# A transformer layer with two kinds of attention: the seam between its expansion stage and its attention stage, rearranged

## The chip, the cores and the metric

The kernel runs on one core of a Trainium2 chip. The metric is the device time of one execution in microseconds (us); the kernel before has a median of 3106.4 us over three runs (3103.69 to 3112.34).

## What is computed

One layer of a diffusion transformer over 2048 latent tokens of width 1024, with 256 context tokens as a prefix. All matrices are float32; the kernel splits operands into a high and a low part (`_hi`, `_lo`) and multiplies them in several passes to keep precision.

```python
u = x * (1 + m1) + m0;  h = u @ w_in                      # modulate, project
mq = rms_norm(h[cq]) @ w_uq                               # MLA queries, 6 heads of 64 + 32 (rope)
kv = rms_norm(h[ckv]) @ w_ukv                             # MLA keys and values, 6 heads
gq, gk = rms_norm(h[gq]), rms_norm(h[gk])                 # GQA, 6 query heads, 2 key heads of 64
q_pe, k_pe, gq, gk = apply_rope(...)
mo = block_attention(mq, m_k, m_v, 6)                     # softmax(q k^T * scale) v, 2304 keys
go = block_attention(gq, g_k, g_v, 2)
co = cb * short_conv(cc * ch, w_conv)                     # depthwise, width 3
y  = concat([mo, go, co]) @ w_o
x  = layer_norm(ALPHA * x + m2 * y)
x  = layer_norm(ALPHA * x + m5 * (relu((x*(1+m4)+m3) @ w1)**2 @ w2))
```

## The kernel before

The program is a row of stages, each a block in which the five engines (PE, ACT, DVE, POOL, SP) run streams written out by hand and meet through semaphores; a block ends for all engines together. `stage_modulate` and `stage_project` come first and leave their results in DRAM. The change touches the next two.

**`stage_expand` (line 616)** computes the MLA queries, keys and values from the compressed rows. It loops over four blocks b of 512 tokens (`NQB`). In each, PE makes three query tiles into the PSUM tile `ring`, then two rope tiles into `rope_ps` (12 matmuls), then three key tiles into `ring`, then, for b below 3, six value tiles (`VG`) into the two banks of `v_ps`. ACT copies each tile out as its high part (`item`, line 696; `values`, 703), DVE subtracts for the low part (731). For the rope tiles DVE multiplies by cosine and sine (749 to 752), POOL adds and subtracts (721, 722), ACT makes `ro_hi` (714), POOL `ro_lo` (725). SP stores everything to DRAM: `store_set` for queries and keys (`qn`, `kn`, line 662), `qr` (679), `vm` (682). It also loads what is missing: compressed rows, tables, and at b = 2 the first GQA head (`load_heads`: `gq`, `gk_ll`, `gv`; lines 842 to 844). A copy into a buffer waits on ACT or POOL until the store that last used it has landed. At the end SP waits for the landing of all stores and of the head's loads (from line 684 on), and so the block ends after them.

Beside this, 40 maxima are taken: softmax of the first attention block needs row maxima of its scores beforehand, so PE multiplies 128 queries by up to 512 keys into a bank (785) and DVE reduces it (737). All of them use the one bank `mx_ps`, except the last ten, which follow everything else in the two `v_ps` banks (`PLACES`, `ALONE`, `last_maxima`). The first needs `gq_first`, loaded late in the stage before.

**`stage_attend` (line 891)** runs 24 blocks of 1024 queries: two GQA blocks and two MLA blocks for each of six heads. A block has 18 steps kt. In each, PE makes scores into one of two pairs of banks (`scores`, 1419), ACT takes the exponential into one of ten probability tiles `pf` (1256), POOL or DVE adds it to a running denominator (1211, 1297); after each six steps PE multiplies the six tiles by the values (1435). Between the score matmuls stand the maxima of the blocks to come (`pair`, 1373, read by DVE in 1275); block 0 carries 27 of them, and from the twentieth on they are on MLA data, for which PE waits on `in_mh`. The negative maximum enters the scores as one more row, laid by `lay_first_row` (1384) for block 0 and by `turn_row`, an ACT copy and small DMAs (`move_row`) for the others. In some blocks (0 among them) PE also multiplies a strip of `w_ada` (`modulations`, 850) after step 11.

SP issues in this order before its loop: the shared rope keys `rk_hh` (four issues) and `rk_lm` (two), `load_m(0)` (the 22 high loads, 14 low loads and values of MLA head 0), `load_part(0)`, `load_wa(0)` (2 MB), `load_part(1)` (convolution inputs). POOL first fills pads of `max_row[1]`, `rk_lm` and `mq` (1159), eight operations, and PE and the row moves wait for all of them (`padded`).

The SBUF of the expansion's own tiles is used again by tiles of attention, `pf` and `rk_lm` among them.

## Time and profile before

| | us |
|---|---|
| median of three runs | 3106.4 |
| the profiled execution | 3108.44 |
| its span (first to last record) | 3106.6 |
| PE busy in the span | 2943.1 (95%) |
| DVE busy | 2291.2 (74%) |
| ACT busy | 1320.4 (43%) |
| POOL busy | 1399.5 (45%) |
| expansion, first to last matmul | 423 to 510 |
| attention, first work | 526.1 |

Times in the rows further down are us from the start of the span. PE is busy nearly everywhere, so what matters are the few stretches where it is not, and its clock: PEclk is the granted TensorE clock as a share of 2.4 GHz, 0.50 being 1.2 GHz. The DMA share is the mean busy share of the 16 DMA engines and can read a little over 1. A line with an idle time in brackets names what ended that idle time.

### The profile page before, as it was taken

How to read it: one execution, taken by the hardware profiler on the slowest of the kernel's cores; microseconds unless marked ns; L12 is line 12 of the kernel's file. 1: busy time of each engine (PE TensorE's matmuls, PEld its weight loads, DVE VectorE, ACT ScalarE, POOL GpSimd, SP SyncE). 2: the span in 40 equal slices, each digit the busy share in tenths (PEclk: the TensorE clock that was granted, in tenths of full speed). 3: DMA queues.
4: the chain of work that ended last, by engine and by line, in shares of the span. 5: the costliest groups of instructions: out<-in, count | busy, mean ns of one | idle time of the engine just before them, and what ended most of it. 6: DMA issues, size and time to landing. Idle time of an engine off the chain costs nothing. (4 is left out here: it accounts for less than half of the span.)

```text
span 3106.6 us, 43125 instructions
## 1 busy us (share of the span) xinstructions
PE 2943.1 (95%) x15760; PEld 2210.2 (71%) x15760; DVE 2291.2 (74%) x3178; ACT 1320.4 (43%) x1891; POOL 1399.5 (45%) x837
## 2 busy tenths in 40 slices
PE   5999966999999999999999969999999999999997
PEld 3889854566656556565657858887788888887886
DVE  4445454778787878878776888776877768888878
ACT  3222323344444444444442445555555544433441
POOL 1233313577786968766661234333333134223420
PEclk7999987999999999999999989999999999999999
DMA  6132379335343243433026876446444488887873
GB/s 257 59 89 76 98 244 274 103 70 130 93 108 86 52 92 84 90 93 76 8 95 237 287 275 242 157 152 263 179 152 157 172 324 302 293 294 293 296 289 141
DMA packets 252012, 526.64 MB, mean 170 GB/s; under 512 B 35568, under 2 KB 110832, under 8 KB 240624
## 3 DMA queue, kind: packets, MB, share of 16 engines
q1 hardware_dynamic: 245296, 498.33, 49.7%
q10 hardware_dynamic: 6528, 25.82, 2.1%
q8 instruction: 115, 1.88, 0.2%
q14 instruction: 73, 0.60, 0.1%
HBM read 363.19 MB, written 160.76 MB: 169 GB/s over the span
## 5 line engine op out<-in xcount | busy, mean ns | idle before, releaser
L1275 DVE TENSOR_REDUCE h_mpart<-a_mx 128x1 f32<-128x512 f32 x920 | 537.8, 632 | 169.4 <-PE a_mx L1373 156.6
L1211 POOL TENSOR_TENSOR a_acc_p<-a_acc_p,a_pf 128x1024 f32<-128x1024 f32 x240 | 578.7, 2411 | 166.8 <-ACT a_pf L1256 139.6
L1256 ACT ACTIVATE a_pf<-o_y 128x1024 f32<-128x1024 f32 x432 | 442.0, 1026 | 398.1 <-PE o_y L1419 392.6
L2430 PE MATMUL f_bank<-slots,f_wx 128*128 128x512 f32 x2304 | 532.8, 391 | 14.7 <-DMA slots<-s_uc 9.2
L2438 PE MATMUL f_bank<-slots 128*128 128x512 f32 x2352 | 539.5, 391 | 3.6 <-DVE slots L2209 3.6
L2438 PEld LDWEIGHTS f_bank<-slots 128*128 128x128 f32 x2352 | 443.4, 189 | 96.5 <-DVE slots L2209 4.3
L2430 PEld LDWEIGHTS f_bank<-slots,f_wx 128*128 128x128 f32 x2304 | 434.8, 189 | 107.6 <-DMA slots<-s_uc 11.2
L2376 POOL TENSOR_TENSOR f_work<-raw_rows 128x512 f32<-128x512 f32 x160 | 220.9, 1382 | 379.5 <-DVE f_wx L2202 367.7
L2385 POOL TENSOR_TENSOR f_y<-f_y,raw_rows 128x1024 f32<-128x1024 f32 x72 | 195.3, 2713 | 343.5 <-DMA raw_rows<-in_w 343.5
L2223 DVE TENSOR_TENSOR f_work<-f_work,f_bank 128x512 f32<-128x512 f32 x256 | 174.4, 681 | 134.1 <-ACT f_work L2101 123.3
L553 PE MATMUL p_main<-win_hi,u_hi 128*128 128x512 f32 (+2 forms) x528 | 197.9, 375 | 15.1 <-PEq L75 14.4
L2209 DVE TENSOR_TENSOR slots<-f_y,slots 128x1024 fp32r<-128x1024 f32 x98 | 151.3, 1544 | 64.1 <-ACT slots L2085 63.1
L553 PE MATMUL p_main<-win_hi,u_lo 128*128 128x512 f32 (+2 forms) x528 | 196.3, 372 | 0.0
L553 PE MATMUL p_main<-win_lo,u_hi 128*128 128x512 f32 (+2 forms) x528 | 196.2, 372 | 0.0
L1435 PE MATMUL a_o<-a_pf,a_v 128*64 128x512 f32 x864 | 192.8, 595 | 0.0
L1435 PE MATMUL a_o<-a_pf,h_gv 128*64 128x512 f32 x864 | 192.8, 595 | 0.0
L2085 ACT ACTIVATE slots<-f_y 128x1024 fp32r<-128x1024 f32 x98 | 104.0, 1061 | 197.5 <-POOL f_y L2385 186.4
L883 PE MATMUL o_y<-slots,low 128*128 128x512 f32 x768 | 180.2, 394 | 3.4 <-PEq L893 3.4
L2207 DVE TENSOR_TENSOR slots<-raw_rows,slots 128x1024 fp32r<-128x1024 f32 x98 | 159.6, 1628 | 25.9 <-ACT slots L2077 25.4
L883 PEld LDWEIGHTS o_y<-slots,low 128*128 128x128 f32 x768 | 143.9, 189 | 34.8 <-issue 5.4
L1419 PE MATMUL o_y<-h_gq,h_gk_hh 64*128 64x512 f32 x864 | 165.5, 406 | 0.2
L2202 DVE TENSOR_TENSOR f_wx<-f_work,f_wx 128x512 fp32r<-128x512 f32 x160 | 162.5, 1017 | 0.6
(279 smaller groups left out, 5101.1 us busy)
## 6 DMA issues: line engine op xcount, KB each, us to landing
raw_rows<-s_hx SPq DMA_DIRECT2D x112, 512.0 KB, 4.0
f_y<-in_w SPq DMA_DIRECT2D x104, 512.0 KB, 5.3
raw_rows<-in_w SPq DMA_DIRECT2D x72, 512.0 KB, 5.8
raw_rows<-in_w SPq DMA_DIRECT2D x32, 1024.0 KB, 4.9
s_hx<-stream SPq DMA_DIRECT2D x128, 256.0 KB, 2.7
s_hx<-f_work SPq DMA_DIRECT2D x96, 256.0 KB, 2.0
raw_rows<-in_w_ada SPq DMA_DIRECT2D x8, 2048.0 KB, 8.4
low<-s_mix SPq DMA_DIRECT2D x32, 512.0 KB, 5.6
```

Of the source, the lines that this page charges most:

```text
L553: mm = nc.tensor.matmul(main[:, b, 0:cn], lhs[s][:, k], rhs[:, k, c0:c0 + cn], start=(k == 0 and rhs is w_hi and lhs is u_hi), stop=(k == ...
L883: mm = nc.tensor.matmul(y[:, half, :], x_[s % 2][:, k], w_[k][:, half * 512:(half + 1) * 512], start=(k == 0 and n == 0), stop=(k == KD - ...
L1211: nc.gpsimd.tensor_tensor(acc[:, :], left[:, :], pf[(b * KT + kt) % NPF][:, :], ALU.add).then_inc(added_p, 1)
L1256: nc.scalar.activation(pf[n % NPF][:, :], sc[n % 2][:, :], ACT.Exp, scale=SCALES[0 if is_mla(b) else 1]).then_inc(exped, 1)
L1275: nc.vector.reduce_max(mpart[b % 2][:, s + 4 * half, k:k + 1], bank(("pair", c), half)[:, 0:CHUNKS[k][1]], AX.X).then_inc(mx_read, 1)
L1419: mm = nc.tensor.matmul(sc[n % 2][:, half * QB:(half + 1) * QB], w, y[strip, :], start=(m == 0), stop=(m == len(ops) - 1))
L1435: mm = nc.tensor.matmul(o_ps[half * DH:(half + 1) * DH, :], v[0 if is_mla(b) else 1][:, kt], pf[n % NPF][:, half * QB:(half + 1) * QB], st ...
L2223: nc.vector.tensor_tensor(t, t, bank[:, (NP * n + pos) % 8, :], plus(sign)).then_inc(c_set, 1)
L2376: nc.gpsimd.tensor_tensor(out, w1_part(n, first), w1_part(n, second), plus(sign)).then_inc(sum_set, 1)
L2385: nc.gpsimd.tensor_tensor(y1[cc % YN], y1[cc % YN], y2[k % Y2N], plus(sign)).then_inc(y_sum, 1)
L2430: mm = nc.tensor.matmul(by_pair(bank[:, m % 8, :]), w[:, k], x[s][:, :, k * P:(k + 1) * P], start=(k == 0 and j == 0), stop=(k == 3 and j ...
L2438: mm = nc.tensor.matmul(bank[:, 4 * (pr % 2) + tt, :], x[s][:, f, tok], y[s][:, 2 + f, :], start=(start and j == 0), stop=(stop and j == 2))
```

## The change

It does the following, in the expansion:

- PE makes the rope tiles first in each block, DVE multiplies them first, ACT makes `ro_hi` before the key tiles, and SP stores `qr` between the query and the key tiles.
- The maxima turn over three banks (`mx_ps` and the two of `rope_ps`): the query half of a block stays on one, keys and values use all three. Six of the last ten move into the ring of block 3, four remain at the end.
- In block 3 SP issues the `qn` stores and stops. The stores of `qr` and `kn` of that block are issued by attention's SP (`last_expanded`). Nobody waits for landings at the end of the block.
- The values `gv` are no longer among the first head's loads.

And in attention:

- The store semaphores live on. ACT waits for `vm` stores before probability tile 2, for `qr` before tile 5, for the others before tile 8; the ten tiles are taken in another order. PE waits for `gv` before its first value product and for the head's loads after `lay_first_row`.
- SP's order is: `gv`, the four stores, `load_wa(0)`, `load_part(0)`, `load_part(1)`, a wait for the landing of all stores, `rk_hh`, the 22 high loads of MLA head 0; then, after the row move of block 1, `rk_lm` and the low loads with the values.
- POOL fills the `rk_lm` pads after its eighth addition of block 0; GQA blocks no longer wait for pads.

```diff
@@ -632,13 +632,19 @@
...
-        first_heads_in, heads_in = g.first_heads_in, sem("heads_in")
+        g.seam = ExitStack()
+        lasting = lambda n: g.seam.enter_context(nc.semaphore("e_" + n))
+        first_heads_in, heads_in = g.first_heads_in, lasting("heads_in")
...
-        st_stored = [sem(f"st_stored{i}") for i in range(2)]
-        rope_done, rope_mults, rope_set, rope_hi, rope_lo, rope_stored = (sem(n) for n in (
-            "rope_done", "rope_mults", "rope_set", "rope_hi", "rope_lo", "rope_stored"))
+        st_stored, rope_stored = [lasting(f"st_stored{i}") for i in range(2)], lasting("rope_stored")
+        rope_done, rope_mults, rope_set, rope_hi, rope_lo = (sem(n) for n in (
+            "rope_done", "rope_mults", "rope_set", "rope_hi", "rope_lo"))
...
-        v_stored = [sem(f"v_stored{i}") for i in range(2)]
+        v_stored = [lasting(f"v_stored{i}") for i in range(2)]
+        g.st_stored = [(st_stored[0], 32 * NQB), (st_stored[1], 32 * (NQB + 1))]
+        g.ro_stored = [(rope_stored, 32 * NQB)]
+        g.v_stored = [(v_stored[i], 16 * ((NVG + 1 - i) // 2)) for i in range(2)]
+        g.heads_in = heads_in
@@ -647,12 +653,16 @@
...
-        ALONE = 10
-        PLACES = [(0, "ring")] * ITEMS + [(0, "v")] * VG + [(1, "ring")] * ITEMS + [(1, "v")] * VG + [(2, "v")] * VG + [(3, "end")] * ALONE
+        ALONE = 4
+        PLACES = [(0, "ring")] * ITEMS + [(0, "v")] * VG + [(1, "ring")] * ITEMS + [(1, "v")] * VG + [(2, "v")] * VG + [(3, "ring")] * ITEMS + [(3, "end")] * ALONE
...
-        mx_bank = lambda c: v_ps[:, c % 2, :] if c in last_maxima else mx_ps[:, :]
+        turning = [bank for b in range(NQB) for where, n in (("ring", ITEMS), ("v", VG), ("end", ALONE)) if (b, where) in PLACES
+                   for bank in ([0] * 3 + [1, 2, 0] if where == "ring" else [(1 + i) % 3 for i in range(n)])]
+        mx_bank = lambda c: mx_ps[:, :] if turning[c] == 0 else rope_ps[:, turning[c] - 1, :]
+        former = lambda c: max((n for n in range(c) if turning[n] == turning[c]), default=-1)
+        on_rope_before = lambda b: max((n for n, (at, _) in enumerate(PLACES) if at < b and turning[n]), default=-1)
@@ -668,25 +678,28 @@
...
+                if b == NQB - 1:
+                    break
+                sp.wait_ge(rope_lo, b + 1)
+                for half, t in enumerate((ro_hi, ro_lo)):
+                    sp.dma_start(g.qr[half][:, :, b * QB:(b + 1) * QB].rearrange("s p t -> p s t"), raw(t[:, :, :])).then_inc(rope_stored, 16)
...
-                sp.wait_ge(rope_lo, b + 1)
-                for half, t in enumerate((ro_hi, ro_lo)):
-                    sp.dma_start(g.qr[half][:, :, b * QB:(b + 1) * QB].rearrange("s p t -> p s t"), raw(t[:, :, :])).then_inc(rope_stored, 16)
...
-            sp.wait_ge(st_stored[0], 32 * NQB)
-            sp.wait_ge(st_stored[1], 32 * (NQB + 1))
-            sp.wait_ge(rope_stored, 32 * NQB)
-            for s in range(2):
-                sp.wait_ge(v_stored[s], 16 * ((NVG + 1 - s) // 2))
-            sp.wait_ge(heads_in, 16 * LOADS_REST)
+
+        def last_expanded(eng):
+            for half, t in enumerate((ro_hi, ro_lo)):
+                eng.dma_start(g.qr[half][:, :, T - QB:T].rearrange("s p t -> p s t"), raw(t[:, :, :])).then_inc(rope_stored, 16)
+            for half, t in enumerate((st_hi, st_lo)):
+                eng.dma_start(g.kn[half][:, KEYS - QB:KEYS].rearrange("(c p) t -> p c t", p=P), raw(t[:, 1, :, :])).then_inc(st_stored[1], 16)
+        g.last_expanded = last_expanded
@@ -706,12 +719,13 @@
...
+                    if c == 3:
+                        act.wait_ge(rope_set, b + 1)
+                        need(act, rope_stored, 32 * b)
+                        nc.scalar.activation(ro_hi[:, :, :], ro[:, :, :], ACT.Copy).then_inc(rope_hi, 1)
...
-                act.wait_ge(rope_set, b + 1)
-                need(act, rope_stored, b * 32)
-                nc.scalar.activation(ro_hi[:, :, :], ro[:, :, :], ACT.Copy).then_inc(rope_hi, 1)
@@ -738,9 +752,6 @@
...
-                for c in range(3):
-                    item(items_before(b) + c, 0, c)
-                    read_maxima(maxima_at(b, "ring", c))
@@ -751,6 +762,9 @@
...
+                    item(items_before(b) + c, 0, c)
+                    read_maxima(maxima_at(b, "ring", c))
+                for c in range(3):
@@ -779,9 +793,9 @@
...
-                    if c == last_maxima[0]:
-                        pe.wait_ge(v_set, VG * NVG)
-                    need(pe, mx_read, c - 1 if c in last_maxima else c)
+                    if turning[c]:
+                        pe.wait_ge(rope_mults, PLACES[c][0] + 1)
+                    need(pe, mx_read, former(c) + 1)
@@ -791,13 +805,14 @@
...
+                need(pe, rope_mults, b)
+                need(pe, mx_read, on_rope_before(b) + 1)
+                products(rope_ps[:, 0, :], q_parts(b, 384))
+                products(rope_ps[:, 1, :], q_parts(b, 512)).then_inc(rope_done, 1)
...
-                need(pe, rope_mults, b)
-                products(rope_ps[:, 0, :], q_parts(b, 384))
-                products(rope_ps[:, 1, :], q_parts(b, 512)).then_inc(rope_done, 1)
@@ -815,8 +830,8 @@
...
-LOADS_REST, LOADS_FIRST = 7, 4
-LOADS_G = LOADS_REST + 2
+LOADS_REST, LOADS_FIRST = 6, 4
+LOADS_G = LOADS_REST + 3
@@ -841,7 +856,11 @@
...
-    eng.dma_start(g.gv[:, :, :], g.vg[kv]).then_inc(done, 16)
+
+
+def load_values(eng, g, h, done):
+
+    eng.dma_start(g.gv[:, :, :], g.vg[h // (HG // HKV)]).then_inc(done, 16)
@@ -931,6 +950,8 @@
...
+        pf = [pf[i] for i in (2, 3, 7, 8, 9, 6, 4, 5, 1, 0)]
+        PF_AFTER = {2: g.v_stored, 5: g.ro_stored, 8: g.st_stored}
@@ -997,6 +1018,12 @@
...
+        in_g_of = lambda h: 16 * (1 + LOADS_G * h)
+
+        def landed(eng, stores):
+            for stored, count in stores:
+                eng.wait_ge(stored, count)
+
@@ -1032,25 +1059,23 @@
...
-            for n in range(4):
-                sp.dma_start(raw(rk_hh[ROPE * n:ROPE * (n + 1), :]), g.kpe[0]).then_inc(in_mh, 16)
-            for strip in STRIPS:
-                sp.dma_start(raw(rk_lm[strip.start:strip.start + ROPE, :]), g.kpe[1]).then_inc(in_ml, 16)
-
-            def load_m(h):
+            def queries(strip, half, which, first, source, done):
+                for blk in range(NBLK):
+                    at = blk * BLK + half * QB
+                    to = slice(strip.start + first, strip.start + first + source.shape[0])
+                    sp.dma_start(raw(mq[blk][to, which, :]), source[:, at:at + QB]).then_inc(done, 16)
+
+            def load_m_hi(h):
...
-
-                def queries(strip, half, which, first, source, done):
-                    for blk in range(NBLK):
-                        at = blk * BLK + half * QB
-                        to = slice(strip.start + first, strip.start + first + source.shape[0])
-                        sp.dma_start(raw(mq[blk][to, which, :]), source[:, at:at + QB]).then_inc(done, 16)
...
+
+            def load_m_lo(h):
+                rows = slice(h * NOPE, (h + 1) * NOPE)
@@ -1089,7 +1114,7 @@
...
-                sp.wait_ge(padded, PADS)
+                sp.wait_ge(padded, PADS if is_mla(b) else PADS - 2)
@@ -1098,19 +1123,26 @@
...
-            load_m(0)
+            load_values(sp, g, 0, in_g)
+            g.last_expanded(sp)
+            load_wa(0)
...
-            load_wa(0)
...
+            landed(sp, g.st_stored + g.ro_stored + g.v_stored)
+            for n in range(4):
+                sp.dma_start(raw(rk_hh[ROPE * n:ROPE * (n + 1), :]), g.kpe[0]).then_inc(in_mh, 16)
+            load_m_hi(0)
...
-                    load_m(i)
+                    load_m_hi(i)
+                    load_m_lo(i)
...
+                    load_values(sp, g, i + 1, in_g)
@@ -1124,6 +1156,10 @@
...
+                if b == 0:
+                    for strip in STRIPS:
+                        sp.dma_start(raw(rk_lm[strip.start:strip.start + ROPE, :]), g.kpe[1]).then_inc(in_ml, 16)
+                    load_m_lo(0)
@@ -1138,7 +1174,7 @@
...
-            sp.wait_ge(in_g, 16 * LOADS_G * (HM - 1))
+            sp.wait_ge(in_g, in_g_of(HM - 1))
@@ -1152,13 +1188,18 @@
...
-            pads = 0
-            for strip in STRIPS:
-                rest = slice(strip.start + ROPE, strip.stop)
-                for tile, fill in [(max_row[1][strip, :], 0.0), (rk_lm[rest, :], 1.0)] + [(mq[blk][rest, R_HM, :], 0.0) for blk in range(NBLK)]:
-                    nc.gpsimd.memset(raw(tile), fill).then_inc(padded, 1)
-                    pads += 1
-                    pool.wait_ge(padded, pads)
+            rest = [slice(strip.start + ROPE, strip.stop) for strip in STRIPS]
+            pads = [(max_row[1][strip, :], 0.0) for strip in STRIPS]
+            pads += [(mq[blk][part, R_HM, :], 0.0) for part in rest for blk in range(NBLK)]
+            for n, (tile, fill) in enumerate(pads):
+                nc.gpsimd.memset(raw(tile), fill).then_inc(padded, 1)
+                pool.wait_ge(padded, n + 1)
+
+            def pad_rope_keys():
+                landed(pool, g.st_stored)
+                for n, part in enumerate(rest):
+                    nc.gpsimd.memset(raw(rk_lm[part, :]), 1.0).then_inc(padded, 1)
+                    pool.wait_ge(padded, PADS - 1 + n)
@@ -1193,6 +1234,7 @@
...
+            PAD_STEP = 8
@@ -1209,6 +1251,9 @@
...
+                    if b == 0 and j == PAD_STEP:
+                        pool.wait_ge(added_p, j)
+                        pad_rope_keys()
@@ -1247,6 +1292,8 @@
...
+                    if n in PF_AFTER:
+                        landed(act, PF_AFTER[n])
@@ -1361,8 +1408,8 @@
...
-                    else:
-                        need(pe, in_g, 16 * LOADS_G * head_of(b))
+                    elif head_of(b):
+                        pe.wait_ge(in_g, in_g_of(head_of(b)))
@@ -1413,7 +1460,8 @@
...
-                        pe.wait_ge(padded, PADS)
+                        if is_mla(b):
+                            pe.wait_ge(padded, PADS)
@@ -1431,6 +1479,8 @@
...
+                    if b == 0:
+                        pe.wait_ge(in_g, in_g_of(0))
@@ -1461,6 +1511,7 @@
...
+            pe.wait_ge(g.heads_in, 16 * LOADS_REST)
@@ -1492,6 +1543,7 @@
...
+    g.seam.close()
```

## Rows read from the trace of the kernel before

**Rows 1.** Windows by stage; columns: window, length, busy us (count) by engine, clock, DMA share, GB/s

```profile
511.00:526.10 15.10, 0.00 (x0) 0.00 (x0) 0.00 (x0) 1.06 (x1) 2.35 (x2) 0.50 0.83 317
...
526.10:540.00 13.90, 10.45 (x50) 8.65 (x52) 7.15 (x12) 4.88 (x5) 9.15 (x10) 0.51 0.97 205
...
540.00:559.00 19.00, 19.00 (x120) 10.65 (x118) 14.00 (x25) 9.14 (x10) 16.67 (x8) 1.00 1.05 223
```

**Rows 2.** Timeline of the seam: start, length, engine, line, operation, [idle before <-releaser]

```profile
499.06 6.59 SPq L662 DMA_DIRECT2D s_qn<-e_st_hi  x1
...
505.69 3.54 SPq L662 DMA_DIRECT2D s_qn<-e_st_lo  x1
...
509.89 0.42 DVE L737 TENSOR_REDUCE h_mpart<-e_v 128x1 f32<-128x256 f32 x1 [0.21 <-PE e_v L785]
...
516.00 0.56 SPq L679 DMA_DIRECT2D s_qr<-e_ro_lo  x1
...
533.95 0.80 PE L1419 MATMUL o_y<-h_max_row,ones_f 64*128 64x512 f32 x2 [1.81 <-POOL a_mq L1159]
...
536.91 1.02 ACT L1256 ACTIVATE a_pf<-o_y 128x1024 f32<-128x1024 f32 x1 [1.11 <-PE o_y L1419]
...
542.15 1.03 ACT L1256 ACTIVATE a_pf<-o_y 128x1024 f32<-128x1024 f32 x1 [0.47 <-PE o_y L1419]
```

**Rows 3.** Waits of the SP queue, 400 to 600: total us, times, longest

```profile
SPq L688 <- DMA s_qr<-e_ro_lo: 8.9, 1, 8.9
```

**Rows 4.** Timelines of DVE and PE at the seam into the expansion

```profile
422.24 0.27 DVE L483 TENSOR_TENSOR k_lo<-tr_k,k_hi 32x128 fp32r<-32x128 f32 x1
...
423.05 0.55 PE L768 MATMUL e_ring<-e_ckv_hi,low 128*128 128x256 f32 x1 [4.23 <-PEq L213]
```

**Rows 5.** Timeline of PE: the modulations of block 0, and of a later block

```profile
566.50 3.30 PE L850 MATMUL a_mx<-raw_rows,cond_pad 128*32 128x512 f32 x16 [2.50 <-DMA raw_rows<-in_w_ada]
...
753.61 1.92 PE L850 MATMUL a_mx<-raw_rows,cond_pad 128*32 128x512 f32 x16
```

**Rows 6.** Timeline of PE: first maximum on MLA data

```profile
572.08 0.61 PE L1373 MATMUL a_mx<-a_nk_hh,a_mq 64*128 64x512 f32 x2
```

**Rows 7.** Timeline of PE in expansion blocks 0 and 1

```profile
430.50 0.79 PE L785 MATMUL e_mx<-h_gk_hh,e_gq_first 128*128 128x512 f32 x1 [2.95 <-DMA e_gq_first<-s_qg]
...
465.94 0.50 PE L785 MATMUL e_mx<-h_gk_hh,e_gq_first 128*128 128x512 f32 x1 [2.16 <-DVE h_mpart L737]
...
472.99 0.50 PE L785 MATMUL e_mx<-h_gk_hh,e_gq_first 128*128 128x512 f32 x1 [0.26 <-DVE h_mpart L737]
...
474.27 0.50 PE L785 MATMUL e_mx<-h_gk_hh,e_gq_first 128*128 128x512 f32 x1 [0.26 <-DVE h_mpart L737]
...
474.61 0.51 PE L768 MATMUL e_v<-low,e_ckv_hi 128*128 128x384 f32 x2
...
474.96 0.34 PE L768 MATMUL e_v<-low,e_ckv_lo 128*128 128x384 f32 x1
```

**Rows 8.** Timeline of ACT in expansion block 0

```profile
440.04 1.33 ACT L696 ACTIVATE e_st_hi<-e_ring 128x512 fp32r<-128x512 f32 x2 [3.92 <-DMA s_kn<-e_st_lo]
```

**Rows 9.** Windows of 1 or 2 us, columns as in rows 1

```profile
456.00:458.00 2.00, 1.61 (x7) 1.00 (x7) 1.67 (x3) 0.60 (x1) 1.08 (x1) 1.00 0.28 73
...
468.00:470.00 2.00, 1.09 (x6) 0.66 (x4) 1.41 (x3) 0.49 (x1) 0.00 (x0) 1.00 0.37 138
...
478.00:480.00 2.00, 2.00 (x10) 1.67 (x9) 1.20 (x2) 0.69 (x2) 1.25 (x1) 1.00 0.49 127
...
506.00:507.00 1.00, 1.00 (x2) 0.55 (x2) 0.79 (x2) 0.00 (x0) 0.00 (x0) 0.50 0.97 157
...
518.00:520.00 2.00, 0.00 (x0) 0.00 (x0) 0.00 (x0) 0.00 (x0) 0.00 (x0) 0.50 1.05 409
...
522.00:524.00 2.00, 0.00 (x0) 0.00 (x0) 0.00 (x0) 0.00 (x0) 0.00 (x0) 0.50 0.40 140
...
560.00:562.00 2.00, 2.00 (x12) 0.68 (x10) 1.89 (x2) 0.00 (x0) 0.00 (x0) 1.00 1.04 384
```

## The prediction, made before the changed kernel ran

> **What bounds the kernel now.** I read the windows of each stage first. Between the last matrix work of the expansion and the first of attention there are 15.1 us with no PE, no DVE and hardly anything else, while the DMA engines are 83% busy [rows 1]. The timeline shows why [rows 2]: DVE reads its last maximum at 509.89 (0.42 us), but the SP queue is still issuing stores; the last one goes out at 516.00 and takes 0.56 us, and SP then waits 8.9 us for it to land [rows 3]. Attention begins at 526.1. A block end alone does not cost this: at the seam before, DVE's last operation (422.24) and PE's first matmul (423.05) lie 0.8 us apart [rows 4], though the loads issued there for the expansion are not waited for. So the stall is a wait for stores.
>
> Behind the seam PE runs at the lower clock for nearly all of 13.9 us (granted 0.51), then at the full one [rows 1]. It waits 1.81 us for POOL's pads [rows 2], and 2.50 us for `w_ada`, which was issued last but for one load; the 16 matmuls of that row then take 3.30 us, against 1.92 us for the same 16 at full clock [rows 5]. After 572 everything is steady. I therefore measure the change at one marker: the first MLA maximum, PE at 572.08 [rows 6]. It lies in block 0, behind every wait named, and the work after it is unchanged; what the marker gains, the kernel gains.
>
> **Part 1, inside the expansion.** Rope first and three banks for maxima.
> - The same matmuls, DVE and ACT operations run, so no busy time changes. With one bank a V tile and its maximum take 1.28 us (maxima start at 472.99 and 474.27) and PE waits for DVE in each [rows 7]. With three banks a tile costs what PE streams: two products start in 0.35 us (474.61, then 474.96), so three take 0.52 and the maximum, a third wider, 0.23: 0.75, say 0.78. 0.5 x 6 = 3.0 us in block 1, which also loses its 2.16 us wait in the ring [rows 7]: 5.2. Block 2: 3.0. Block 3: 1 (six maxima leave the tail, but `ro_hi`, about 1 us, now precedes the keys on ACT).
> - Block 0: PE's 2.95 us wait for `gq_first` is covered by 12 rope products. The keys still wait for the context store until 440.04 [rows 8], but PE, with three banks and rope behind it, has them and the first V tile ready by then, and DVE has its rope products behind it: about 4 us by a walk through the order, 0 at worst. Sum 5.2 + 3 + 1 + 4 = 13.2 us: compute would end at 510.3 - 13.2 = 497.1.
> - The new ACT wait, `rope_set` and `rope_stored` ahead of key item 3, queues three key copies behind it. DVE's rope products and POOL's two operations behind them now come first in the block, so they are done when ACT is at item 3; the rope stores of the block before go ahead of the head loads, no longer behind them. I take 0; the other bound is the 8.9 us that a wait for such a store lasted [rows 3], and it would be hidden behind SP as far as 6.6 us (part 2).
>
> **Part 2, the SP queue.** The expansion now ends for SP with the two `qn` stores of block 3. Those issues took 6.59 and 3.54 us, ending at 509.2, since the queue was full [rows 2]. The DMA engines were saturated from 458 to 522.7 but for dips: shares 0.28, 0.37 and 0.49 in three windows of 2 us, together 3.7 us idle of 6 and some tenths beside them, 4.0 [rows 9]. Compute that runs ahead fills these: 4.0 us. `gv` (0.59 MB) moves behind the seam: 1.5 us at the 409 GB/s of stores [rows 9]. So SP ends at 509.2 - 5.5 = 503.7, later than compute's 497.1: SP's issues decide, and most of part 1 is hidden. With 0.6 us of barrier, attention starts at 504.3, not 526.1: 21.8 us.
>
> **Part 3, attention up to the marker.** GQA no longer waits for pads: 1.85. Clock at the start: an exponential and the wait before it take 2.13 us at the lower clock (536.91) and 1.50 at the full one (542.15) [rows 2]; without the pad wait in the ramp I take two such steps back, 1.4 (bounds: 0, and 4 for six). `w_ada` is issued fifth, lands in time: 2.5 for the wait and 3.30 - 1.92 = 1.4 for the clock [rows 5]. Sum 7.15. PE could be at the marker at 572.08 - 21.8 - 7.15 = 543.1.
> - `pf` waits: the sixth probability tile needs `qr`, which part 4 has landed by 516 to 518; the tile is due some 13.5 us after the start, about 518: 0 to 1. The ninth needs `kn`, with 9 us to spare. The two late pad memsets (2 x 2 us) stand in POOL behind its eighth addition and ahead of three that PE's denominators need only a block later: 0.
>
> **Part 4, what becomes late next: the MLA loads.** The marker needs the 26 loads of `in_mh`, 3.4 MB (4 x 0.29, 2 x 0.59, 4 x 0.13 and 16 x 0.03, by their shapes). They were issued first; now they follow `gv`, four stores, 2.1 MB of `w_ada`, 1.05 MB of convolution and a wait for the stores. Volumes from the DMA side: old end of stores 522.7, less `kn` and `qr` (2.36 MB, 5.8 us), less `gv` 1.5, less 4.0 reclaimed: `qn` is out at 511.4. Then `gv` 1.5, four stores 5.8, `w_ada` 5.4 and convolution 2.7 at the 384 GB/s of such loads [rows 9]: 526.8. Then 3.4 MB at the 205 to 223 GB/s that the same loads had [rows 1], 16.2 us, and 2.5 us to be seen (bytes ended at 522.7, the wait at 525.4 [rows 3, 9]): 545.5. SP's own issuing (26 issues of about 0.5 us, from the landed wait at about 521) is done before that. So PE waits 2.4 us at the marker, and the clock falls as after the equal wait for `w_ada`; 1.0 for that (it cost 1.4 there [rows 5]). The low half (3.1 MB) has 60 us until block 2: 0.
>
> The rate of the stores is where the Trainium skill speaks against this. The rows show 409 GB/s with the engines full. The page "DMA: Bandwidth & Descriptors", section Specifications, gives an HBM limit per core of about 358 GB/s; by it, an estimate, the bytes between 504 and 526.8 would take 2.5 us more, and the marker would gain 2.5 us less. The trace disagrees with the page, so the sum goes by the row.
>
> **Sum.** Marker 572.1 to 545.5, less 1.0: 25.6 us. The profiled execution took 3108.44 (span 3106.6 and 1.8 around it): 3082.8. It lies 2.0 above the median 3106.4, which gives 3106.4 - 25.6 = 3080.8, my prediction.
>
> **Rivals.**
> - A, SP or the expansion gives nothing (queue full as before): the start is at 509.9, the marker PE-bound at 548.7, gain 23.4 or, if the clock also comes back 5 us later than taken, 18: 3083 to 3088. For it: SP's issues were blocked by loads that remain. 0.25.
> - B, DMA is slower: loads and stores at about 300 GB/s instead of 409 up to 526.8, as in the mixed windows, give 7 to 10 us more: gain 14 to 18, 3088 to 3092. 0.1.
> - C, faster: MLA loads at over 250 GB/s land by 542, the marker is free at 543 or, if the issues are not held, at 540: gain 29 to 33, 3073 to 3077. 0.12.
> - D, the seam still waits for its stores (a block end that drains them): start at 511.4 + 2.5 + 0.6 = 514.5, gain 18.4, 3088. Against it: rows 4. 0.03.
> - E, slower than before: the same queue, at the marker. If all 12.5 MB issued or pending at 504 crawl at 157 GB/s, the lowest rate shown by a full queue [rows 9], they take 79.6 us: landed at 586.4, gain -14.3 - 1.0, 3121.7. It decides once `in_mh` lands after 571, a mean rate below 195 GB/s. Against it: stores and `w_ada` never ran so slowly. 0.03.
>
> **Numbers.** The forecast with its neighbourhood, 0.47: 3077 to 3084. The range takes in A, D and most of B and C: 3073 to 3092. A measurement of this kernel tells 0.3% (9 us) from no change. Faster by more: forecast, A, C, D and B nearly whole, 0.94; within 0.3%: 0.03; slower: 0.03.
>
> **What would show it.** Right: first attention work between 502 and 507; no SP wait for a landing before it; no PE wait for POOL or `w_ada` in block 0; a PE wait of 1 to 5 us for MLA loads at the first MLA maximum, the lower clock after it; V tiles 0.8 us apart in expansion blocks 1 and 2. Wrong: a PE wait at the marker over 8 us, ACT waiting for `rope_stored` in the expansion, `gv` late at the first V batch, or a start after 512.

## The result, and the profile after

The changed kernel takes 3079.9 us (median of six runs, 3072.1 to 3088.4); the kernel before, measured beside it, 3103.7 (3100.5 to 3112.3). The ratio is 0.9925, with a 95% interval of 0.9907 to 0.9943. The gain is 23.7 us where 25.6 were forecast, and the time 3079.9 where 3080.8 was, inside the range. Its parts did not all come out as forecast.

| us | before | after |
|---|---|---|
| profiled execution | 3108.44 | 3088.39 |
| span | 3106.6 | 3086.6 |
| PE busy | 2943.1 | 2937.5 |
| first key product of the expansion | 423.05 | 422.03 |
| first attention work | 526.1 | 497.5 |
| first MLA maximum (the marker) | 572.08 | 547.49 |
| end of attention block 0 (first copy of `o`) | 587.5 | 564.9 |

Busy times have hardly moved, as they should: only waits were removed. The profiles start the expansion up to 4 us apart, though the code ahead of it is the same in all kernels, so from here on I count from its first key product, the 423.05 of [rows 4]. The marker then comes at 149.0 before and 125.5 after.

The windows of the stretch after (window, length, busy us by PE, PEld, DVE, ACT, POOL with counts, granted clock, DMA share, GB/s) show the hole of [rows 1] gone, and another one opened further back:

```profile
458.00:478.00 20.00, 19.26 (x85) 14.94 (x84) 14.98 (x25) 10.54 (x20) 7.34 (x4) 1.00 1.05 359
478.00:498.00 20.00, 14.59 (x64) 11.02 (x62) 13.95 (x27) 6.28 (x11) 5.30 (x6) 1.00 1.05 336
498.00:518.00 20.00, 16.96 (x92) 11.57 (x94) 11.78 (x20) 8.04 (x8) 11.06 (x10) 0.74 1.04 376
518.00:538.00 20.00, 19.82 (x127) 10.03 (x125) 14.19 (x23) 6.17 (x6) 14.80 (x7) 1.00 1.06 221
...
538.00:546.00 8.00, 0.65 (x6) 0.21 (x2) 0.97 (x4) 1.02 (x1) 2.34 (x1) 0.77 0.62 103
```

The DMA engines are now full from 458 to 538 without a dip, where before they had several [rows 9]. PE is idle for over 7 of the 8 us from 538 on. The timeline of the changed kernel (start, length, engine, line, operation, idle before and its releaser) has the seam and that second hole:

```profile
492.22 4.90 SPq L672 DMA_DIRECT2D s_qn<-e_st_lo  x1
...
496.74 0.41 DVE L751 TENSOR_REDUCE h_mpart<-e_rope 128x1 f32<-128x256 f32 x1
497.52 0.10 POOL L1189 MEMSET a_cp<- 128x1 f32 x1 [3.23 <-POOLq L618]
...
499.17 1.97 PE L1431 MATMUL a_mx<-minus_ident_r,low 128*128 128x128 f32 x8 [2.51 <-DVE low L1329]
...
503.01 0.79 PE L1420 MATMUL a_mx<-h_gk_hh,h_gq 64*128 64x512 f32 x2 [1.87 <-DMA h_gk_ll<-s_kg]
...
547.49 0.80 PE L1420 MATMUL a_mx<-a_nk_hh,a_mq 64*128 64x512 f32 x2 [8.84 <-DMA a_mq<-s_qr]
```

SP ends its last `qn` issue at 497.1 and DVE its last maximum at 497.15: SP and compute reach the block's end together, and attention begins 0.4 us later, so a block end without a landing to wait for costs next to nothing, as [rows 4] had said. The last row answers to [rows 6]: the first MLA maximum has an 8.84 us wait for MLA queries in front of it that was not there before. POOL's pads and `w_ada`, which [rows 2, 5] had as waits, are gone from the list of waits.

The landings of the loads in the two traces, which no row above shows, give the limit of the gain. In the kernel before, the last of the 26 loads that the marker needs landed at 126.5 us from the first key product, 22.5 us before PE was there. In the changed kernel it lands at 125.4. SP issues these loads behind 3.15 MB more than before, but it starts earlier (the first one at 94.4, not 103.1), so in time they are hardly moved: what changed is that PE now gets there first.

### The profile page after: what moved, and what is told of

The parts are those of the page before. It is cut to its first block and busy times, and to the rows that moved or that the text cites. A ratio compares the mean times of both kernels' runs of the same rounds, so it can differ in the third digit from the quotient of the medians.

```text
span 3086.6 us, 43133 instructions
## 1 busy us (share of the span) xinstructions
PE 2937.5 (95%) x15760; PEld 2210.5 (72%) x15760; DVE 2286.3 (74%) x3178; ACT 1319.0 (43%) x1891; POOL 1398.1 (45%) x837
## 5 line engine op out<-in xcount | busy, mean ns | idle before, releaser
L2275 DVE TENSOR_TENSOR f_work<-f_work,f_bank 128x512 f32<-128x512 f32 x256 | 174.4, 681 | 133.2 <-ACT f_work L2153 122.4
```

## The experiments

My theory, from the prediction's part 4: the first MLA maximum is held by the DMA queue, whose loads the change has pushed back in SP's order, so what shortens or lengthens PE's own way to it counts only in part, and what lies ahead of those loads counts in full. Its rival: PE's own way sets the time, and each part of the change is worth what it moves the start of attention by. All were compared with the kernel before in the same set of runs. The whole time scatters by some 10 us from run to run, and the profiles show where: from the first matmul on `f_wx` to the end the three profiles of the changed kernel take 1260.8, 1262.2 and 1250.4 us, in code that no experiment touches. So the table gives both: the ratio of whole times, and, from each kernel's one profile, the start of attention on PE (its first matmul), the marker and the end of block 0, in us from the first key product. The three rows of the changed kernel say how far such a number repeats: 2 us at the end of block 0, 5 at the marker, 7 at the start.

| kernel | start | marker | end of block 0 | median, us | ratio to before (95%) |
|---|---|---|---|---|---|
| before | 104.7 | 149.0 | 164.4 | 3104 | 1 |
| changed | 77.1 | 125.5 | 142.9 | 3079.9 | 0.9925 (0.9907 to 0.9943) |
| changed, second | 83.0 | 126.1 | 143.2 | 3080.3 | 0.9925 (0.9904 to 0.9947) |
| changed, third | 76.0 | 121.4 | 141.6 | 3078.3 | 0.9919 (0.9903 to 0.9935) |
| landing wait back | 95.2 | 132.2 | 147.6 | 3086.1 | 0.9946 (0.9928 to 0.9964) |
| old expansion | 91.7 | 128.9 | 144.4 | 3084.1 | 0.9939 (0.9923 to 0.9954) |
| both back | 101.0 | 137.4 | 152.8 | 3093.4 | 0.9967 (0.9955 to 0.9980) |
| one bank | 88.3 | 129.0 | 146.2 | 3088.3 | 0.9951 (0.9935 to 0.9968) |
| convolution late | 80.5 | 122.7 | 139.9 | 3082.9 | 0.9928 (0.9910 to 0.9947) |
| `w_ada` late, blocks 1, 2, 4 | 78.8 | 115.2 | 129.9 | 3084.1 | 0.9936 (0.9916 to 0.9956) |
| `w_ada` late, odd blocks | 78.4 | 114.9 | 129.5 | 3065.6 | 0.9874 (0.9860 to 0.9889) |
| the same, old expansion | 89.4 | 124.3 | 138.9 | 3077.4 | 0.9915 (0.9896 to 0.9933) |
| the same, landing wait back | 95.2 | 130.2 | 144.7 | 3077.5 | 0.9911 (0.9891 to 0.9930) |

**The changed kernel again**, twice, without an edit.

> The changed kernel itself, timed on the chip that the next three share. Theory S (the seam's landing wait is what the change removes, and the MLA loads that it pushes back are the next bound): about 24 us below the kernel before, a PE wait of 3 to 9 us for a_mq at the first MLA maximum, and the times scattered by as much as that wait varies. Rival R (the scatter of 16 us between the runs shown has nothing to do with the seam): the PE wait at the marker is the same as in the first profile (8.8 us) whatever the time.

> The changed kernel once more, on the chip of the next three. Theory S: the first MLA maximum at 547 to 548 on PE, after a wait for a_mq of 5 to 9 us, as in both profiles so far; the time within 3072 to 3092, since what scatters lies behind attention.

The waits at the marker were 8.84, 5.87 and 6.92 us. The slowest and the fastest of the three profiled executions, by the span 3087.1 and 3077.4, differ by 12 us behind the start of the MLP and by 2 at the end of block 0. The scatter of the whole time is not the seam's; what causes it in the MLP was not tried. That the wait is the same whatever the time (the rival) was not quite so either: it varies by 3 us, but not with the time. It is the distance between PE's arrival (116.6, 120.2 and 114.5) and the last landing (125.4, 126.0 and 121.4), and both move from profile to profile.

**The landing wait put back.** The last stores are issued by the expansion's SP, and it waits for all:

```diff
+            sp.wait_ge(rope_lo, NQB)
...
+            sp.wait_ge(lo_set, items_before(NQB - 1) + 6)
...
+            for stored, count in g.st_stored + g.ro_stored + g.v_stored:
+                sp.wait_ge(stored, count)
+            sp.wait_ge(heads_in, 16 * LOADS_REST)
...
-            g.last_expanded(sp)
```

> Last stores issued by the expansion's SP again and all landings awaited there; all else as changed. Theory S: DMA was saturated from 442 on, the qn stores are through at about 508, kn and qr at about 514, seen at 517; attention starts at 517.5 instead of 497.5. Then gv, w_ada, convolution and MLA loads follow, 9.1 MB less the stores: the marker comes at 517.5 + 38.9 = 556 from PE or 517.5 + 9.6 + 18.5 + 2.5 = 548 from DMA, so PE-bound at 556 instead of 547.5, PE not waiting there: 6 to 9 us slower than the changed kernel, not the 20 us by which the start moves. Rival R1 (the start decides, nothing new became late behind it): 20 us slower than the changed kernel, no gain left over the kernel before but pads and w_ada, about 5 us.

Waits of the SP queue in that kernel, 480 to 560 (total us, times, longest), and PE's marker in its timeline:

```profile
SPq L703 <- DMA s_qr<-e_ro_lo: 5.7, 1, 5.7
SPq L704 <- DMA s_kn<-e_st_lo: 3.8, 1, 3.8
```

```profile
554.74 0.61 PE L1428 MATMUL a_mx<-a_nk_hh,a_mq 64*128 64x512 f32 x2
```

Attention starts 12 to 19 us later than in the changed kernel (95.2 against 76.0 to 83.0), and block 0 ends only 5.0 us later (147.6 against a mean of 142.6). The marker's row has no bracket: PE does not wait there, the MLA loads are in since 124.8. So in the changed kernel the end of block 0 goes by the loads, not by the start; had the start set it there, it would have moved by all of the 12 to 19. Here PE's own way sets it.

**The old expansion order with the new seam.** PE and DVE take rope after the queries, ACT makes `ro_hi` after the values, SP stores `qr` behind the loads, maxima stay on one bank and ten of them come at the end (on the two rope banks, where the kernel before had the `v_ps` banks):

```diff
-        ALONE = 4
-        PLACES = ... + [(2, "v")] * VG + [(3, "ring")] * ITEMS + [(3, "end")] * ALONE
+        ALONE = 10
+        PLACES = ... + [(2, "v")] * VG + [(3, "end")] * ALONE
...
-                   for bank in ([0] * 3 + [1, 2, 0] if where == "ring" else [(1 + i) % 3 for i in range(n)])]
+                   for bank in ([1, 2] * 5 if where == "end" else [0] * n)]
...
```

> The expansion's old order (rope tiles after the queries, ro_hi after the values, qr stored behind the loads, maxima on one bank, ten of them at the end, on the rope banks), with the new seam: last kn and qr issued and all landings awaited by their users. Theory O (the new order matters through the chain qr store landed - ro_hi - ro_lo, which would otherwise hold the block's end): ACT waits some 6 to 9 us for the landing of qr again, the expansion ends at 511 to 516, the marker is PE-bound at 550 to 555; 3 to 8 us slower than the changed kernel. Rival Q (the DMA queue binds everything from here to the marker, so that compute's order is hidden): marker within 1.5 us of 547.5.

ACT's timeline there, and PE at the marker:

```profile
506.16 1.06 ACT L727 ACTIVATE e_ro_hi<-e_ro 96x1024 fp32r<-96x1024 f32 x1 [6.21 <-DMA s_qr<-e_ro_lo]
```

```profile
548.83 0.50 PE L1419 MATMUL a_mx<-a_nk_hh,a_mq 64*128 64x512 f32 x2
```

ACT waits 6.2 us for the landing of `qr`, as before the change. The start moves from 76 to 83 back to 91.7. The marker has no wait and comes at 128.9, 4.6 us behind the changed kernel's mean; block 0 ends at 144.4, only 1.8 us behind it. The difference is the clock: without a wait PE needs 15.5 us from the marker to the end of block 0, behind waits of 5.9 to 8.8 us it needs 17.1 to 20.2. So the wait for `qr` is back, but the end of block 0 hardly moves. By the whole times the two can't be told apart (intervals overlap).

**Both put back.**

> Old expansion order and the landing wait, with the changed kernel's loads and pads in attention: what is left of the change without both of its main parts. Each alone costs 1.5 and 4.7 us in the end of block 0. Theory T (either part is enough to bring compute down to the DMA chain, and only both away show what they hide): 154, 11 us later than the changed kernel, more than the sum of the two; the rest of the gain over the kernel before (164.5) is pads, w_ada's place and gv. Rival (the parts add): 149.

152.8 us at the end of block 0. Each part alone costs 1.8 and 5.0 us, their sum would be 149.4; together they cost 10.2. The expectation said 154 against 149 for plain addition, and the run is nearer to the first: the parts stand in for one another. The rest of the way to the kernel before, 11.6 us, is what this kernel still has of the change: its start is 3.7 us earlier (101.0 against 104.7), and from the start to the marker it needs 36.4 us instead of 44.3 (pads, `w_ada`, clock).

**One bank for the maxima of blocks 0 to 2**, all else as changed.

```diff
-                   for bank in ([0] * 3 + [1, 2, 0] if where == "ring" else [(1 + i) % 3 for i in range(n)])]
+                   for bank in ([0] * n if b < 3 else [0] * 3 + [1, 2, 0] if where == "ring" else [(1 + i) % 3 for i in range(n)])]
```

> Maxima of expansion blocks 0 to 2 on one bank as before; all else as changed. Theory S: V tiles take 1.28 us again, compute in the expansion is some 7 us later in sum, but SP's stores and the DMA queue are what was waited for: the marker moves by less than 2 us. Rival (compute ahead of the DMA queue pays): start and marker later by 4 to 7 us.

Here my theory missed: it gave the marker less than 2 us, its rival 4 to 7. The start comes at 88.3, the marker at 129.0, 4.7 us behind the changed kernel's mean of 124.3, and it still has a wait for MLA queries, of 4.0 us. The DMA share is 0.91 and 0.97 in the windows 458:478 and 478:498, where the changed kernel has 1.05 in both. As I read it, compute that lags leaves the DMA engines gaps, and the MLA loads at the other end of the queue come later: the DMA chain is not given, the expansion feeds it. That is a reading, and it has a gap: 3.6 us are lost at the end of block 0, but only 1.0 at the end of block 8 and 0.4 at the end of attention, while the median is 8 us higher. Neither difference was followed up. In the timeline of the changed kernel, the maxima behind the V tiles of block 2 start 0.76 us apart but for one gap of 1.1, against 1.28 in [rows 7]:

```profile
476.15 0.39 PE L799 MATMUL e_rope<-h_gk_hh,e_gq_first 128*128 128x512 f32 x1
476.91 0.40 PE L799 MATMUL e_rope<-h_gk_hh,e_gq_first 128*128 128x512 f32 x1
...
478.79 0.39 PE L799 MATMUL e_rope<-h_gk_hh,e_gq_first 128*128 128x512 f32 x1
479.54 0.40 PE L799 MATMUL e_rope<-h_gk_hh,e_gq_first 128*128 128x512 f32 x1
480.30 0.40 PE L799 MATMUL e_mx<-h_gk_hh,e_gq_first 128*128 128x512 f32 x1
```

**The convolution parts behind the high MLA loads.**

```diff
             load_wa(0)
-            load_part(0)
-            load_part(1)
             landed(sp, g.st_stored + g.ro_stored + g.v_stored)
...
             load_m_hi(0)
+            load_part(0)
+            load_part(1)
```

> The two convolution parts (1.05 MB) issued behind the high MLA loads instead of ahead of them. Theory S (the MLA loads queue behind bytes): they land 2.7 us earlier, the PE wait for a_mq falls from 8.8 to about 6, and the kernel is 2.5 us faster than the changed one. Rival R2 (the loads are late through their own slow rate or through SP's wait for the stores, not through what is queued ahead): no change, within 1 us.

Block 0 ends at 139.9, 2.7 us ahead of the changed kernel's mean and 1.7 ahead of its best profile, about the 1.05 MB's own time (2.7 us in the prediction). It is near the scatter, and the whole time (3082.9) does not show it. By itself inconclusive; the next two are the same test with three times the bytes.

**`w_ada` behind the MLA loads too**, its first use moved from block 0 to block 1.

```diff
-        MOD_BLOCKS = (0, 2, 4, 6, 8, 12, 16, 20)
+        MOD_BLOCKS = (1, 2, 4, 6, 8, 12, 16, 20)
...
-            load_wa(0)
-            load_part(0)
-            load_part(1)
             landed(sp, g.st_stored + g.ro_stored + g.v_stored)
...
             load_m_hi(0)
+            load_wa(0)
+            load_part(0)
+            load_part(1)
```

> w_ada (2.1 MB) and the convolution parts both issued behind the high MLA loads, and the first modulations moved from block 0 to block 1, so that nobody needs w_ada early. Theory S: the MLA loads land 8 us earlier, at about 539; PE is at the marker at about 537 (1.9 us less, the modulations are gone from block 0), waits 1 to 3 us or not at all and keeps its clock: 8 to 10 us faster than the changed kernel, about 32 us faster than the kernel before. Rival R2: PE still waits about 8 us, no gain.

Timelines of PE and SP in that kernel:

```profile
534.90 0.50 PE L1420 MATMUL a_mx<-a_nk_hh,a_mq 64*128 64x512 f32 x2 [0.84 <-DMA a_mq<-s_qr]
...
635.49 3.25 PE L869 MATMUL a_mx<-raw_rows,cond_pad 128*32 128x512 f32 x16 [8.18 <-DMA raw_rows<-in_w_ada]
```

```profile
627.14 0.62 SPq L1088 DMA_DIRECT2D raw_rows<-in_w_ada  x1
```

The marker moves to 115.2 and the end of block 0 to 129.9, 12.7 us earlier. Of that, 3.2 go back in block 1, where the first modulations now stand, and 9.5 are left at its end. Yet the whole time is no better. The second row has the reason, a mistake of mine in the edit: the second set is loaded only when block 1 has been stored, at 627.14, and was now used one block later, in block 2; PE waited 8.18 us and its 16 matmuls then took 3.25 us instead of 1.92 [rows 5]. At the end of block 2 nothing of the 9.5 is left. The gain was made and given away.

**The same with two blocks between the sets.**

```diff
-        MOD_BLOCKS = (0, 2, 4, 6, 8, 12, 16, 20)
+        MOD_BLOCKS = (1, 3, 5, 7, 9, 12, 16, 20)
```

> As the run with the first modulations in block 1, but the first five sets at blocks 1, 3, 5, 7, 9, two blocks apart as before, so that each w_ada load again has its time. Theory S (the marker is bound by bytes ahead of the MLA loads; the run before gave its gain back to the second w_ada load, issued 8 us too late for block 2): marker at 535, block 0's last copy at 549.5 and no PE wait for in_w_ada anywhere; attention ends 12 to 15 us earlier than in the changed kernel, 3066 to 3072 in all. Rival (the gain at the marker is lost again in any case, in the blocks behind): attention ends where that of the changed kernel does.

```profile
534.76 0.51 PE L1420 MATMUL a_mx<-a_nk_hh,a_mq 64*128 64x512 f32 x2 [0.97 <-DMA a_mq<-s_qr]
```

PE waits 0.97 us at the marker and for `in_w_ada` nowhere; attention ends (last copy of `o`) at 1582.5 in its profile, against 1603.2, 1602.4 and 1604.4 in those of the changed kernel. The median is 3065.6 us, ratio 0.9874 (0.9860 to 0.9889; the intervals of this kernel and of the changed one do not touch). This is the version that beats both, by about 14 us over the changed kernel and 38 over the one before.

The whole 14 us is not the queue's. At the end of attention this kernel is 18.2 us ahead of the changed kernel's mean, at the end of block 0 13.1. The other 5 come from where the modulations stand now. With them in the even blocks PE waits for maxima on DVE in blocks 4 and 8, here in the changed kernel:

```profile
688.09 0.50 PE L1420 MATMUL a_mx<-h_gk_hh,h_gq 64*128 64x512 f32 x1 [0.94 <-DVE h_mpart L1322]
...
704.21 0.50 PE L1420 MATMUL a_mx<-h_gk_hh,h_gq 64*128 64x512 f32 x1 [1.93 <-DVE h_mpart L1322]
...
871.01 0.50 PE L1420 MATMUL a_mx<-h_gk_hh,h_gq 64*128 64x512 f32 x1 [1.10 <-DVE h_mpart L1322]
...
886.98 0.67 PE L1420 MATMUL a_mx<-h_gk_hh,h_gq 64*128 64x512 f32 x1 [1.79 <-DVE h_mpart L1322]
```

With them in the odd blocks these four waits, 5.8 us, are gone; the run before, with late `w_ada` but modulations in blocks 4 and 8, still has them (0.93, 1.65, 1.07 and 1.84). What shows that the changed kernel is held by what is queued ahead of the MLA loads is the marker: their last landing moves from 121.4 to 126.0 up to 114.8, and the marker with it. The windows 498:518, 518:538 and 538:546 of this kernel have PE busy 19.5, 19.0 and 8.0 us; in the changed kernel the last one has 0.65:

```profile
498.00:518.00 20.00, 19.48 (x110) 12.41 (x111) 11.58 (x22) 8.03 (x8) 13.10 (x9) 0.84 0.85 304
518.00:538.00 20.00, 19.02 (x120) 10.59 (x116) 16.19 (x27) 8.39 (x9) 15.27 (x8) 1.00 1.03 240
538.00:546.00 8.00, 8.00 (x55) 4.77 (x56) 6.83 (x12) 4.07 (x5) 3.87 (x2) 1.00 0.45 150
```

It is not the end either. The DMA share is 0.62, 0.21 and 0.33 in the three windows of 2 us from 510 to 516: SP issues the MLA loads only once the last store has landed, at 514.3. What a finer wait would give was not tried.

**The two parts of the change once more, now with the MLA loads out of the way.**

> The old expansion order together with w_ada and the convolution behind the MLA loads and the modulations in odd blocks. Measured by the end of attention block 0 (the first copy of o), counted from the first key product of the expansion: 142.9 in the changed kernel, 144.4 with the old expansion alone, 129.5 with the late w_ada alone. Theory T (two chains end at the first MLA maximum, compute and DMA; the new expansion order was hidden behind the DMA chain, and is worth its full size once that is shortened): 143, 13 us later than the late w_ada alone; 12 to 14 us slower than that kernel in all, about 3078. Rival (the expansion order gives nothing in any case): 130 to 132 and about 3067.

> Last stores issued and all landings awaited in the expansion, together with the late w_ada; new expansion order kept. Theory T: the start of attention, about 19 us later, is no longer hidden: end of block 0 at 146 against 129.5, and 16 us slower in all, about 3081, where the same wait cost 5 us with the loads in the order of the changed kernel. Rival (the landing wait costs 5 us, as there, whatever the loads): 135.

The old expansion puts the end of block 0 at 138.9 against 129.5: it costs 9.3 us, where it cost 1.8 with the loads in the changed order. The landing wait puts it at 144.7: it costs 15.2, where it cost 5.0. The start of attention moves by 11.0 and 16.8 us, so nearly all of that now arrives. The whole times follow, 3077.4 and 3077.5 against 3065.6. So either part has several times its former price once the loads are out of the way. The first was expected at 13; 2.3 us of what is missing lie in the start, at 89.4 here and at 91.7 in the old expansion's own run, a difference within that mark's scatter. PE at the marker, with the landing wait back, has no wait:

```profile
552.10 0.62 PE L1428 MATMUL a_mx<-a_nk_hh,a_mq 64*128 64x512 f32 x2
```

## Why the prediction was right

**The picture held.** Two chains end at the first MLA maximum: PE's own, and the DMA queue's. The prediction had PE's at 543.1 and DMA's at 545.5, that is 120.0 and 122.4 from the first key product. The marker came at 125.5, 126.1 and 121.4, bound by DMA in all three: PE was there at 116.6, 120.2 and 114.5. That the landing wait would be traded for a shorter one at MLA loads (part 4) was the main point, and the experiments show it from both sides: give the queue less ahead of the MLA loads and the marker moves by 9 us; delay the start by 12 to 19 us and the end of block 0 moves by 5. Rival A (PE-bound marker) is what happens when either part of the change is undone, not in the changed kernel. Rival D, a block end that drains its stores, is refuted by the 0.4 us between 497.15 and 497.52. Rival E had the right place and a price that was far too high.

Of the signs that the prediction named, most came: no SP wait for a landing before attention, no wait for POOL or `w_ada` in block 0, none for `rope_stored` or `gv`, the lower clock behind the marker. Two did not. Attention's first work came at 497.5 and 498.1 where 502 to 507 was said, and only in the second profile within it, at 503.2. And the wait of 8.84 us lies above the 8 that was to mean "wrong"; the other two, 5.87 and 6.92, lie between the two lines.

**Part 1, the expansion.** Compute was said to end at 497.1, 74.0 from the first key product; DVE ended at 75.1, 81.0 and 74.1 in the three profiles. V tiles at 0.78 us came out at 0.76. That the first and third are so near has luck in it. The 0 for `rope_stored` was right, but there are waits that no term had: copies of ACT wait for landings that they did not wait for before,

```profile
486.40 1.28 ACT L709 ACTIVATE e_st_hi<-e_ring 128x512 fp32r<-128x512 f32 x2 [5.41 <-DMA s_qn<-e_st_lo]
...
492.31 1.57 ACT L709 ACTIVATE e_st_hi<-e_ring 128x512 fp32r<-128x512 f32 x3 [0.47 <-DMA s_kn<-e_st_lo]
```

because compute that runs ahead of a full queue meets its own stores. It was the query and key stores that were late, not the `rope_stored` that I had bounded. In the second profile ACT has three such waits behind the first block (2.92, 4.60 and 2.48 us), and compute is done 6 us later.

**Part 2, SP.** The start of attention was forecast at 504.3, PE's first matmul 1.65 later, 82.9 from the first key product; it came at 77.1, 83.0 and 76.0. "Most of part 1 is hidden" behind SP was wrong as a reason: in all three profiles SP's last `qn` issue and DVE's last maximum end within 0.5 us of each other, and the one-bank run shows that compute's order moves the start by 5 to 12 us: there SP is through with `qn` at 82.4 and DVE with the maxima at 86.3, and with the old expansion it is 82.7 and 87.1. Without the new order compute decides. In the effect on the kernel it was nearly right, since the new order was worth 1.8 us as things stand, 9.3 with the MLA loads early.

**Part 3, from the start to the marker.** Forecast 44.3 less 7.15, 37.2. Where nothing waits at the marker it took 37.0 (landing wait back) and 36.4 (both back). In the changed kernel, less its wait, it took 39.5, 37.2 and 38.5. In the first and third PE waited 1.87 and 1.42 us for `gk_ll`, which an earlier start had overtaken; that wait was not in the prediction.

**Part 4, the size of the wait.** 2.4 us were forecast at the marker, 5.9 to 8.8 measured. In the first profile, with 8.84, PE was there 3.4 us sooner than forecast (116.6 for 120.0) and the loads 3.0 us later (125.4 for 122.4). The term that was too small is the loads' own time. What goes ahead of them was to be through at 526.8 and seen 2.5 us later, 106.3 from the first key product; its last load landed at 106.6, 112.7 and 105.1. From the first landing of the MLA loads to the last it took 20.1, 20.1 and 17.9 us, where their bytes were given 16.2. The rate falls at 522, when `w_ada` is in:

```profile
518.00:520.00 2.00, 2.00 (x12) 0.70 (x10) 0.02 (x1) 0.00 (x0) 1.86 (x2) 1.00 1.06 398
520.00:522.00 2.00, 2.00 (x18) 1.57 (x15) 1.82 (x4) 0.76 (x1) 1.76 (x1) 1.00 1.12 350
522.00:524.00 2.00, 2.00 (x16) 1.16 (x12) 2.00 (x5) 1.29 (x2) 1.66 (x1) 1.00 1.07 139
...
540.00:542.00 2.00, 0.00 (x0) 0.00 (x0) 0.00 (x0) 0.00 (x0) 1.71 (x1) 1.00 0.69 123
542.00:544.00 2.00, 0.00 (x0) 0.00 (x0) 0.00 (x0) 0.00 (x0) 0.00 (x0) 0.60 0.56 96
544.00:546.00 2.00, 0.00 (x0) 0.00 (x0) 0.00 (x0) 0.00 (x0) 0.00 (x0) 0.50 0.24 33
```

The stores and `w_ada` ran at about 400 GB/s, as the row of before had it and not at the 358 that the Trainium skill gives as a core's HBM limit ("DMA: Bandwidth & Descriptors", Specifications). The same page of the Trainium skill says, under Bandwidth, that about 358 GB/s is each core's part when both cores of a pair stream; this kernel runs on one core. The trace decides, and it agreed with the choice made.

From 522 to 546 the engines moved 3.75 MB, the 3.4 and the rest of the convolution, at 156 GB/s and not at 205 to 223. They end with a tail in which the share falls to 0.69, 0.56 and 0.24; I read it as some of the 16 engines having nothing left while others still work. The rates of [rows 1] had other loads beside these in the second window, the low ones from 540.1 on, but that company does not explain the difference. With the landing wait back the same loads stand last in the queue too, and run at 200 GB/s to a short tail, 16.5 us from first landing to last:

```profile
528.00:544.00 16.00, 16.00 (x101) 8.96 (x103) 11.39 (x21) 7.16 (x8) 14.74 (x8) 1.00 1.03 200
544.00:546.00 2.00, 2.00 (x14) 1.02 (x12) 2.00 (x5) 1.60 (x2) 2.00 (x1) 1.00 0.23 40
```

Why the changed kernel is slower at them stays open.

**The clock after the wait** was put at 1.0 us. From the marker to the end of block 0 the kernel before took 15.4 us, the changed one 17.4, 17.1 and 20.2: 1.7 to 4.8. Part 4's stall was short of its size and so was this. The marker gave 24.7 us for 26.6 forecast (149.0 less a mean of 124.3), the clock took 2.8 and not 1.0, and so the end of block 0 gained 21.9 (164.4 less 142.6) for 25.6: there the forecast was 4 us too high.

**Luck in the number.** At the end of attention the gain is 23 us, and the whole time gave 23.7, with an interval of some 18 to 29 that can't tell 21.9 from 25.6. That 3079.9 came within 1 us of the 3080.8 on record is luck: the forecast set out from a median of 3106.4 for the kernel before, which was 3103.7 when measured beside the changed one, and that cancels the missing part of the gain.

## What to carry to other kernels

When a wait for stores at a seam goes, look for who stands behind those stores in the same queue: here the gain stops at the first user of the loads that were pushed back, and a nearly free reorder of those loads by their due times moved that user by 9 us more. When a test moves work as well (here the modulations), follow the marks to the end of the stage, or its side effect is taken for the gain. Parts that shorten one of two chains must be tested together and with the other chain out of the way; alone, either part of this change looked worth 2 to 5 us, and it was 9 and 15 once nothing hid it. Where the whole time scatters by 10 us in a stage that the edit does not touch, compare marks in the profile counted from a common event, and repeat the profile to know how far they hold.

## What the runs showed of the hardware that was not expected

- The issue of a store by SP, 0.3 to 0.6 us when the queue is short, took 4.9 us at 492.22 behind queued loads, with DMA full all along, so that SP reached the block's end no sooner than compute. In the changed kernel `load_wa(0)` and the next issue took 4.17 and 5.07 us in the same way.
- Loads into strips of 32 or 64 partitions kept the DMA share at 1.0 and moved 139 to 228 GB/s, stores and full-width loads 393 to 413 from 502 to 520 at nearly the same share. A full DMA share says little of bytes.
- The clock came back after very different times. In the first profile of the changed kernel, after the 8.84 us wait, PE is at the lower level (1.2 GHz, 0.50) to 552 and back at 2.4 GHz by 554, some 5 us of work:

```profile
548.00:552.00 4.00, 4.00 (x20) 2.76 (x16) 2.42 (x4) 1.02 (x1) 1.30 (x1) 0.50 0.00 0
552.00:554.00 2.00, 2.00 (x15) 1.88 (x15) 0.33 (x2) 1.29 (x2) 1.80 (x2) 0.84 0.00 0
```

In the third one, after a shorter wait (6.92 us), it stays there for nearly all of 546 to 558, though PE is busy throughout:

```profile
546.00:550.00 4.00, 4.00 (x20) 2.75 (x18) 2.58 (x4) 1.24 (x2) 1.68 (x1) 0.50 0.00 0
550.00:554.00 4.00, 4.00 (x19) 3.54 (x20) 1.13 (x3) 1.07 (x2) 3.05 (x2) 0.50 0.02 4
554.00:558.00 4.00, 4.00 (x24) 3.41 (x23) 2.37 (x5) 1.29 (x2) 0.00 (x0) 0.53 0.02 1
```

Why they differ stays open. It makes up part of why the marker came 4.1 us earlier in the third profile and block 0 ended only 1.2 us earlier.
